# The first batch's sixteen cache pages asked for in two groups, each when its place in memory is free

## The reference, cut to what matters

```python
past = cache_nsa_kv[layer, page_table].reshape(B, past_len, 4, NSA_KV_HEADS, HEAD_DIM)
o_cmp, o_sel = nsa_global(q, jnp.concatenate([past, rows.astype(past.dtype)], axis=1), q_pos)
```

```python
act = jax.nn.gelu(jnp.einsum('td,thkd->thk', x, u[eidx]).astype(jnp.float32))
return jnp.einsum('thk,thkd->td', (g * act).astype(x.dtype), v[eidx])
```

## Time and profile before

| | us |
|---|---|
| median of 3 runs | 2901.63 (2890.51 to 2906.18) |
| profiled execution, its own time | 2900.44 |
| its span, first to last instruction | 2898.6 |
| busy: PE / DVE / POOL / ACT | 1481.4 / 2028.9 / 1147.4 / 265.6 |
| DMA | 993 MB, mean 343 GB/s |

### The profile page before, as it was taken

The page is one execution under the profiler, slowest core; times in us unless marked ns, Lnnn a source line. Parts: engine busy times, 40 slices in busy tenths (PEclk is TensorE's granted clock), DMA queues, the critical chain, the costliest instruction groups (busy, mean ns, idle before and its releaser), DMA issues.

```text
span 2898.6 us, 19199 instructions
## 1 busy us (share of the span) xinstructions
PE 1481.4 (51%) x5745; PEld 863.9 (30%) x5745; DVE 2028.9 (70%) x2732; ACT 265.6 (9%) x556; POOL 1147.4 (40%) x644
## 2 busy tenths in 40 slices
PE   7996958788996747057766775237450000000000
PEld 3453742223443427045555564012120000000000
DVE  0123296656886566847778777773688999999998
ACT  1021110000211010011111112000100000000000
POOL 0000012323543232213333433222425888888885
PEclk9998979899998779578888887559685555555555
DMA  8766759997999799569999998669988999999997
GB/s 284 237 221 234 251 198 412 411 411 298 358 404 351 261 383 361 191 261 387 401 391 408 389 388 308 223 213 364 361 334 331 421 422 422 422 422 422 422 422 305
DMA packets 267348, 993.01 MB, mean 343 GB/s; under 512 B 31217, under 2 KB 60598, under 8 KB 183432
## 3 DMA queue, kind: packets, MB, share of 16 engines
q0 software_dynamic: 92160, 671.13, 56.8%
q1 hardware_dynamic: 174072, 319.40, 31.7%
q10 hardware_dynamic: 1040, 1.59, 0.1%
HBM read 980.73 MB, written 19.77 MB: 345 GB/s over the span
## 4 chain that ended last, share of the span: by engine, by line
PE 35%; DMA 21%; POOL 18%; DVE 14%; issue 5%; SPq 4%; ACT 1%; DVEq 0%; POOLq 0%; ACTq 0%
POOL arena L1776 18%; PE ps L751 14%; DMA arena<-in_cache_nsa_kv_dram 6%; PE ps L818 5%; DMA arena<-in_peer_v_dram,arena 5%; DMA arena<-in_w_in_dram 5%; DVE arena L1229 3%; PE ps L371 3%; SPq L580 2%; PE ps L374 2%; SPq L581 2%; PE ps L962 2%; DMA arena<-in_peer_wq_dram 2%; DVE arena L1307 2%; DVE arena L1304 1%
## 5 line engine op out<-in xcount | busy, mean ns | idle before, releaser
L1776 POOL DMA_INDIRECT arena<-in_peer_u_dram,arena x320 | 507.1, 1585 | 1177.8 <-DVE arena L1226 703.6
L1776 POOL DMA_INDIRECT arena<-in_peer_v_dram,arena x320 | 640.1, 2000 | 542.4 <-DVE arena L1229 309.8
L1226 DVE CUSTOM_DVE_ANT_0 arena<-arena 128x2048 bf16<-128x2048 f32 x320 | 733.3, 2292 | 165.0 <-DMA arena<-in_peer_u_dram,arena 148.8
L1229 DVE SCALAR_TENSOR_TENSOR arena<-arena 128x2048 f32<-128x2048 f32 x296 | 696.0, 2351 | 98.8 <-DMA arena<-in_peer_v_dram,arena 59.6
L751 PE MATMUL ps<-arena 128*128 128x512 f32 (+3 forms) x1248 | 554.8, 598 | 59.2 <-DMA arena<-in_w_in_dram 39.4
L751 PEld LDWEIGHTS ps<-arena 128*128 128x128 f32 (+1 forms) x1248 | 211.3, 184 | 373.3 <-issue 347.0
L818 PE MATMUL ps<-arena 128*128 128x512 f32 (+1 forms) x384 | 188.9, 650 | 35.9 <-DMA arena<-in_w_out_dram 35.8
L371 PE MATMUL ps<-arena 128*128 128x128 f32 x512 | 78.6, 330 | 169.9 <-DMA arena<-in_cache_nsa_kv_dram 169.9
L371 PEld LDWEIGHTS ps<-arena 128*128 128x128 f32 x512 | 77.1, 244 | 172.9 <-DMA arena<-in_cache_nsa_kv_dram 172.9
L962 PE MATMUL ps<-arena 128*128 128x128 f32 x1024 | 120.8, 282 | 13.0 <-DMA arena<-in_peer_wq_dram 13.0
L962 PEld LDWEIGHTS ps<-arena 128*128 128x128 f32 x1024 | 120.0, 199 | 13.5 <-DMA arena<-in_peer_wq_dram 13.2
(11 more groups left out here) (333 smaller groups left out, 1544.6 us busy)
## 6 DMA issues: line engine op xcount, KB each, us to landing
arena<-in_w_in_dram SPq DMA_DIRECT2D x96, 1024.0 KB, 5.7
arena<-in_w_out_dram SPq DMA_DIRECT2D x48, 1024.0 KB, 7.0
arena<-in_peer_wq_dram SPq DMA_DIRECT2D x48, 1024.0 KB, 6.8
arena<-in_cache_nsa_kv_dram SPq DMA_DIRECT2D x128, 384.0 KB, 8.6
arena<-in_cache_nsa_kv_dram SPq DMA_DIRECT2D x128, 128.0 KB
arena<-in_state_win_kv_dram SPq DMA_DIRECT2D x32, 256.0 KB, 21.6
out_s_win_dram<-in_state_win_kv_dram SPq DMA_DIRECT2D x1, 8064.0 KB
arena<-in_peer_u_dram,arena POOLq DMA_INDIRECT x320, 10.3
```

The lines of the kernel that those rows point to most:

```text
L1226: nc.vector.tensor_tensor_reduce(out=PROD, in0=rows_in, in1=H[t], scale=1.0, scalar=0.0, op0=ALU.mult, op1=ALU.add, accum_out=DOTS[:, c:c ...
L1229: nc.vector.scalar_tensor_tensor(out=ACC[t], in0=rows_in, scalar=GG[:, t, c:c + 1], in1=ACC[t], op0=ALU.mult, op1=ALU.add).then_inc(g_used, 1)
L1776: nc.gpsimd.indirect_dma_start(BUF[SLOT[p]], None, tables[kind], bass.IndirectOffsetOnAxis(EIDX[:, t, c:c + 1].bitcast(U32), 0)).then_inc( ...
```

## The change

Only the order of SP's requests and waits changes. `pages` gets an argument, the pages to ask for. After the two stores SP no longer waits at once for the new keys and values and for `v_qk`. It waits until the last weights of tile 1's query projection are used (`w_used` at `W1[1] + W_REST`), and asks for pages 6 to 15 of batch 0. It then waits for the last route of tile 1 (`v_route` at 8) and asks for pages 0 to 5. Behind that stand the two waits that stood ahead (`st_kv`, `v_qk`), and then the windows. The pages of all other batches, and all other engines, are as they were.

```diff
-                    sp.wait_ge(st_kv, 16)
-
-                    sp.wait_ge(ld_pt, 16)
-                    sp.wait_ge(v_qk, 9 * 3)
-
-                    def pages(b, part, done):
-                        for g in range(NPAGE):
+                    def pages(b, part, done, which=range(NPAGE)):
+                        for g in which:
...
-                    pages(0, slice(0, 768), pages_in)
+                    sp.wait_ge(ld_pt, 16)
+                    sp.wait_ge(w_used, W1[1] + W_REST)
+                    pages(0, slice(0, 768), pages_in, range(6, NPAGE))
+                    sp.wait_ge(v_route, 8)
+                    pages(0, slice(0, 768), pages_in, range(6))
+                    sp.wait_ge(st_kv, 16)
+                    sp.wait_ge(v_qk, 9 * 3)
                     window(0)
```

## The result

The changed kernel took 2859.45 us (median of 4 runs, 2854.99 to 2865.39), the kernel before 2900.72 (2890.51 to 2906.18). The ratio is 0.9862, 95% interval 0.9833 to 0.9891: 41 us less, between 32 and 48. The prediction was 2864, with a range of 2853 to 2880. The profiled execution took 2862.11 us, with a span of 2859.2.

A forecast was written before the change was run, and what follows sets the result against it. SP's late request for batch 0's pages was taken to bound the kernel. PE gains 36.7 us, early pages and windows cost 0, DVE's takes leave 36.4 to 36.7; 36.5 carried: 2900.4 - 36.5 = 2864 us, range 2853 to 2880.

The forecast's parts named there:

- The path: Chain of waits from DVE's tile 1 routes through SP's page request, 25.07 us landing, to PE's first multiplication at 1258.75 us.
- The ten pages: Pages 6 to 15, requested from about 1159.5 to 1170 us, land long before 1211; cost 0, at most 4.4 us.
- the sharing worked out: Gathers beside the ten early pages keep 304 of 419 GB/s, so 1.8 MB take 1.6 us more, hidden.
- the first rival: The ten early pages lengthen DVE's route chain by 4.4 us, giving 2868 us; chance 0.08.
- The six pages: Pages 0 to 5, requested from 1212.5 us, land in 4.3 us; PE starts at 1222.1, gaining 36.7 us.
- The windows: SP's window requests from 1218.2 us reach PE in time; cost 0, at the longest landing 4.6 us.
- What is late next: DVE's eight takes end by 1244.8 us, PE's scores come at 1244.5; DVE's wait shrinks from 36.40 to 0 to 3.
- Whether it lasts: Later batches shift as a whole, mean period 66.9 us before, so 36.5 us carry through to the end.
- The longer route chain: Rival: the gathers' 5.0 us in hand are used up by the ten pages, `v_route` comes later: 2868 us; chance 0.08.
- Giving back in the batches: Rival: batches at the DMA engines' limit partly return the gain; 15 us kept for certain, 2885 us; chance 0.06.
- The changed order did what it says: Denies the rival that PE's page count still ends late, start within 2 us of 1258.75, 2899 to 2901; chance 0.03.
- The slower rival: Gathers against page requests lengthen each batch; at a 75 us period the time is 2921 us; chance 0.02.

## Why the prediction was right

**The path.** It was read rightly: SP's request stood on the chain, and the moved request shortened it by what was late next allowed. The kernel with all sixteen behind the route shows that the early ten are necessary, the one with the six at the old place that the six set the last few us.

**The ten pages (forecast cost 0, at most 4.4).** Cost 0, but for another reason than the sharing worked out. The prediction misread a row here: its 16.9 us is the middle of two gathers, the second with 16.1 and the third with 17.6, so the third had 4.3 us in hand and not 5.0, and the first rival's 4.4 us should have been 5.1. The third gather was forecast to land up to 1.6 us later. It landed as before, 17.5 us after its request for 17.6, since hardly any page data flowed by then, and not from 1161 us on: in the trace the first packet of a page's row (3072 bytes) starts at 1166.8 us, 0.6 us before this landing, and ahead of it SP's queue still moves the packets of its own two stores (6144 and 4096 bytes). The first page landed 8.2 us after its request at 1161.3. The gathers that stood beside the pages' data are later ones, asked for at 1169.6, with 10.4 us to landing, where their counterparts of the kernel before took 7.5; the next takes begin only at 1189.96, so they had some 10 us in hand. The changed kernel, second and third gather together (16.0 and 17.5), then the one asked for at 1169.6; then the kernel before, at 1168.1:

```profile
DMA to landing us min/median/max: 16.0/16.8/17.5
...
DMA to landing us min/median/max: 10.4/10.4/10.4
```

```profile
DMA to landing us min/median/max: 7.5/7.5/7.5
```

The rule of the Trainium skill that was weighed there ("DMA: Bandwidth & Descriptors", section "Queues, rings and completion order"), engines taking turns between queues a packet at a time, fits the second pair of numbers and could not show in the first. The trace of the kernel before bears it out too: from 1234 to 1247 us, with gathers and pages both waiting, the gathers' queue has 543 packets and SP's 540.

**The six pages (forecast: PE's start 10.7 us behind the route end).** It came 12.0 and 11.1 us behind. The sum of the first is 0.7 us to the first request (1.1 taken), five more requests of 1.10 us each (1.056 taken), and 5.8 us to the last landing (4.3 taken). So the landing is the term that was too small, by 1.5 us. The first gather of the stage is not the cause: none of its packets moves before 1226 us in the trace, and the page landed at 1224.9. What does move beside the last page's packets, from 1221 us on, are the packets of the windows asked for right behind it (2048 bytes). The fifth page, which had landed at 1222.2, took 4.2 us. So the windows are the likely cause; no experiment moved them alone. Changed kernel, the first and the last of the six from request:

```profile
DMA to landing us min/median/max: 3.2/3.2/3.2
...
DMA to landing us min/median/max: 5.8/5.8/5.8
```

**The windows (0, at most 4.6).** No cost where it was looked for: PE has no wait between L374 and L387 that names them, and its scores came 1246.35 - 1224.90 = 21.5 us after its start, for 22.45 before, as L371 took 9.24 us for 10.24. That the stage's gain meets the forecast within 0.2 us is in part luck: this 1.0 us makes up for most of the 1.3 us by which PE started late.

**What is late next.** Forecast: PE and DVE meet, DVE's wait is 0 to 3 us. Measured: 2.33 and 1.33. The kernel with fourteen early pages shows that both were close: with PE 5.4 us earlier, the scores are used only 3.2 us earlier, as DVE's takes are then late.

**Whether it lasts.** The rest of the run, from the first use of the scores to the end, takes 1599 to 1623 us in all kernels. For the seven that leave the copy alone it is 1609 to 1623, with the kernel before at 1617 and the two traces of the changed one on either side of it. Nothing systematic is given back in the batches. This scatter of some 13 us, not the stage, is why single medians of the changed kernel read 30 and 41 us. The forecast of 36.5 is the stage's gain; that the first median lay 5 us below the forecast is scatter.

**The rivals.** The longer route chain did not come, even with twice the traffic: 45.9 us from the third pair's takes to the end of the last route in all eleven traces. Giving back in the batches did not come: mean period 66.4 us. The changed order did what it says. The slower rival, a longer period, did not come either.

## What to carry to other kernels

A request that stands behind a wait it does not need is worth the time until the next thing is late, so work out what is next late first: here DVE's 36.4 us of idle time, nearly all of which came back with ten of sixteen pages early, and 3 us more with fourteen. Of a group that is awaited as a whole, only the last one's landing counts: let as few as possible be asked for late, and into an empty queue. Idle DMA time is free only for transfers that share it well with what is in flight: 7.9 MB of pages cost nothing there, while 8.26 MB in eight long rows cost 24 us of PE's start.

## What was not expected of the hardware

A copy from input to output in eight rows of 1 MB ran at 230 GB/s with the DMA engines at a share of 0.53, and made gathers beside it land after 35 us; cut into sixteen parts per row it ran at 372 GB/s and a share of 1.02. And a page asked for while gathers and SP's own stores were in flight took 8.2 us to land, one asked for in an empty queue 3.2.
